# Prompt attention of a hybrid decoder layer: heads in groups of 4, 2, 1 and 1, the causal mask added by a product, ScalarE making all copies of turned probabilities

## Chip, cores and metric

The kernel runs on one core of one Trainium2 chip. The metric is the device time of one execution in microseconds, as the median of several runs.

## The reference, cut to what matters

One layer of a decoder is computed for a prompt of 512 tokens and for 8 sample tokens with a paged past. For the prompt, 16 heads (8 of a latent attention with 96 query values, 8 of a forgetting attention with 64) attend causally over at most 512 keys:

```python
qb = min(Q_BLOCK, T)                       # 128 queries at a time, 4 blocks
...
mask = k_pos[None, :] <= pos[:, None]
s = jnp.where(mask[None, None], s, NEG_INF)
p = jax.nn.softmax(s, axis=-1)
return jnp.einsum('bhqs,bshd->bqhd', p.astype(v.dtype), v)
```

After it come two norms, the output projection, and an expert layer that gathers rows of two large tables. All arithmetic is float32.

## The kernel before, in words

The five engines run programs written out by hand, with a semaphore for each kind of step; within one engine the order of the code is the order of the work. The stages are: projections and attention of the sample rows and of the four prompt blocks b = 0 to 3 (up to about 431 us of the profile), then output projection, routing, and the gathers of expert rows (GpSimd starts each gather, VectorE and TensorE use the rows), with the work on the paged past of the sample tokens between them.

For each prompt block TensorE projects the normed rows (line 1368), turns queries and keys into QT and KT (line 1412), and then goes through 16 heads. For block b there are w = 128(b+1) keys. A head costs:

- scores (line 1422): one float32 product with w columns into PSUM bank 2 or 3, in turn by the head's number. Each float32 product appears as two MATMUL instructions; a transpose appears as one.
- VectorE adds the causal mask to the last 128 columns (line 976, followed by a wait of the engine for itself) and takes the negated row maximum (line 978).
- ScalarE takes the exponential with the maximum as its bias, and sums the row in the same instruction (line 614). It goes to Pm, two buffers.
- TensorE turns the probabilities, b+1 transposes of 128x128, into bank 4 or 5 (line 1430).
- the turned probabilities are copied to SBUF into PT, two buffers: for even heads by VectorE (line 972), for odd heads by ScalarE (line 607).
- values (line 1437): b+1 products with 64 columns, two instructions each, into banks 0 and 1.

TensorE's order is: scores of head hh+1, turn of head hh, values of head hh-1. ScalarE's order is: exponential of hh, and then the copy of hh-1 when that head is odd. VectorE's is the same with mask, maximum and copies of even heads.

Between the heads of blocks 0 to 2 lies a part of the next block's start: x_squares(t+1) on ScalarE after head 4 (line 552), x_mean(t+1) on VectorE after head 5, rms (two small activations, lines 542 and 543) on ScalarE after head 6, x_scale(t+1) on VectorE after head 7 (lines 831 to 834 and 868; it waits for rms), turn_x(t+1) on TensorE after head 10 (8 transposes, line 1349), x_gain(t+1) on VectorE after head 12 (line 875). Block 3 has none of these.

When block 3's last values are done (semaphore o_ps), SyncE loads the last five of eight pieces of w_o (line 403), for which the output projection waits.

Of the kernel before, what the change touches and what calls it, by code (L numbers as in the profile page):

```python
# [18 lines left out]
ALU = mybir.AluOpType  # L19
ACT = mybir.ActivationFunctionType  # L20
AX = mybir.AxisListType
# [4 lines left out]
P = 128  # L26
# [3 lines left out]
NB = T // P  # L30
# [7 lines left out]
VD = 64  # L38
R = 128
FD = 64  # L40
KM = NOPE + RP
KF = FD + 2
# [14 lines left out]
CW = PAST // NCH  # L57
K_V0, K_U1, K_V1, K_U2 = range(0, 12), range(12, 36), range(36, 52), range(52, 64)
V_U2, V_V2, V_U3 = range(0, 6), range(6, 16), range(16, NPG)

TAIL_QPE, TAIL_CKV, TAIL_KPE, TAIL_F = 0, 256, 384, 416
TAIL = 424
# [4 lines left out]
C_ID, C_MASK, C_TRI, C_ONES, C_COS, C_SIN, C_DIM, C_IOTA, C_END = 0, 128, 256, 384, 512, 592, 672, 706, 722  # L67
# [4 lines left out]
def build(nc, x_prompt, x_sample, w_in, w_k, w_v, w_kT, w_o, w_q, sub_keys, gains, g_cols, g_ffn, consts, dec_consts,  # L72
# [3 lines left out]
    with ctx:  # L76
# [3 lines left out]
        def sem(name):  # L80
            return ctx.enter_context(nc.semaphore(name))
# [26 lines left out]
        Pm = part(160, 1024).rearrange("p (i n) -> p i n", i=2)  # L108
        PT = part(164, 1024).rearrange("p (i n) -> p i n", i=2)
# [71 lines left out]
        con = sb("con", [P, C_END])  # L181
# [13 lines left out]
        nmx = sb("nmx", [P, 16])  # L195
        rs = sb("rs", [P, 16])
# [13 lines left out]
        ps = ctx.enter_context(nc.psum_tensor("ps", [P, 8, 512], F32))  # L210
        ident = con[:, C_ID:C_ID + P]
# [49 lines left out]
        s_ps = sem("s_ps")  # L261
        max_done = sem("max_done")
        exp_done = sem("exp_done")
        pT_ps = sem("pT_ps")
        pT_done = [sem("pT_done_even"), sem("pT_done_odd")]
        o_ps = sem("o_ps")
        mx_done = sem("mx_done")
        mixT_done = sem("mixT_done")
# [85 lines left out]
        def _(sp):  # L354
# [172 lines left out]
        def _(act):  # L527
# [29 lines left out]
            for t, b in enumerate(ORDER):  # L557
# [42 lines left out]
                    nc.scalar.activation(dst, src, ACT.Copy).then_inc(qk_even, 1)  # L600
                w = (b + 1) * P

                def copy_pT(hh):
                    act.wait_ge(pT_ps, 16 * b + hh + 1)
                    if 16 * b + hh >= 2:
                        act.wait_ge(o_ps, 16 * b + hh - 1)
                    nc.scalar.activation(PT[:, hh % 2, 0:w], ps[:, 4 + hh % 2, 0:w],
                                         ACT.Copy).then_inc(pT_done[1], 1)

                for hh in range(16):  # L610
                    act.wait_ge(max_done, 16 * b + hh + 1)
                    if 16 * b + hh >= 2:
                        act.wait_ge(pT_ps, 16 * b + hh - 1)
                    nc.scalar.activation(Pm[:, hh % 2, 0:w], ps[:, 2 + hh % 2, 0:w], ACT.Exp,
                                         bias=nmx[:, hh:hh + 1], accum_out=rs[:, hh:hh + 1]
                                         ).then_inc(exp_done, 1)
                    if hh and (hh - 1) % 2:
                        copy_pT(hh - 1)

                    if t < NB and hh == 4:  # L620
                        x_squares(t + 1)
                    if t < NB and hh == 6:
                        rms(P, 1)
                copy_pT(15)
                act.wait_ge(mx_done, b + 1)
                act.wait_ge(o_ps, 16 * (b + 1))
# [187 lines left out]
        def _(dve):  # L814
# [9 lines left out]
            def step(ins):  # L824
                dve.wait_ge(v_step, after(ins))
# [59 lines left out]
            for t, b in enumerate(ORDER):  # L885
# [79 lines left out]
                    V_.tensor_copy(dst, src).then_inc(qk_odd, 1)  # L965
                w = (b + 1) * P

                def copy_pT(hh):
                    dve.wait_ge(pT_ps, 16 * b + hh + 1)
                    if 16 * b + hh >= 2:  # L970
                        dve.wait_ge(o_ps, 16 * b + hh - 1)
                    V_.tensor_copy(PT[:, hh % 2, 0:w], ps[:, 4 + hh % 2, 0:w]).then_inc(pT_done[0], 1)

                for hh in range(16):
                    dve.wait_ge(s_ps, 16 * b + hh + 1)
                    step(V_.tensor_tensor(ps[:, 2 + hh % 2, b * P:w], ps[:, 2 + hh % 2, b * P:w],
                                          con[:, C_MASK:C_MASK + P], ALU.add))
                    V_.tensor_reduce(nmx[:, hh:hh + 1], ps[:, 2 + hh % 2, 0:w], AX.X, ALU.max,
                                     negate=True).then_inc(max_done, 1)
                    if hh and (hh - 1) % 2 == 0:  # L980
                        copy_pT(hh - 1)

                    if t < NB and hh == 5:
                        x_mean(t + 1)
                    if t < NB and hh == 7:
                        x_scale(t + 1)
                    if t < NB and hh == 12:
                        x_gain(t + 1)
                dve.wait_ge(o_ps, 16 * (b + 1))
# [352 lines left out]
        def _(pe):  # L1342
# [19 lines left out]
            for t, b in enumerate(ORDER):  # L1362
# [52 lines left out]
                pe.wait_ge(qk_odd, 4 * (b + 1))  # L1415
                w = (b + 1) * P

                def scores(hh):
                    kd = KM if hh < 8 else KF
                    if hh >= 2:  # L1420
                        pe.wait_ge(exp_done, 16 * b + hh - 1)
                    T_.matmul(ps[:, 2 + hh % 2, 0:w], QT[0:kd, hh, :], KT[0:kd, hh, 0:w],  # L1422
                              start=True, stop=True).then_inc(s_ps, 1)

                def turn(hh):
                    pe.wait_ge(exp_done, 16 * b + hh + 1)
                    if hh >= 2:
                        pe.wait_ge(pT_done[hh % 2], 8 * b + hh // 2)
                    for a in range(b + 1):
                        last = T_.transpose(ps[:, 4 + hh % 2, a * P:(a + 1) * P], Pm[:, hh % 2, a * P:(a + 1) * P],  # L1430
                                            ident)
                    last.then_inc(pT_ps, 1)

                def values(hh):
                    pe.wait_ge(pT_done[hh % 2], 8 * b + hh // 2 + 1)
                    for a in range(b + 1):
                        last = T_.matmul(ps[:, hh // 8, VD * (hh % 8):VD * (hh % 8) + VD],  # L1437
                                         PT[:, hh % 2, a * P:(a + 1) * P], V[:, a, VD * hh:VD * hh + VD],
                                         start=(a == 0), stop=(a == b))
                    last.then_inc(o_ps, 1)  # L1440

                scores(0)
                for hh in range(16):
                    if hh + 1 < 16:
                        scores(hh + 1)
                    turn(hh)
                    if hh:
                        values(hh - 1)
                    if t < NB and hh == 10:
                        turn_x(t + 1)  # L1450
                values(15)
            turn_mixture(NB - 1)


# [465 lines left out]
```

## Time and profile before

| | |
|---|---|
| median of 3 runs | 2458.63 us (2458.03 to 2470.38) |
| span of the profiled execution, first to last instruction | 2563.8 us |
| PE (TensorE matmul) busy | 1793.9 us, 70% |
| DVE (VectorE) busy | 1169.1 us, 46% |
| ACT (ScalarE) busy | 348.5 us, 14% |
| mean granted clock of TensorE | 0.817 of full speed |

Of the profiled execution the span is all that was recorded; no time of its own stands beside it. It is 105 us longer than the median of the runs without a profile. In the profile PE is the matmul part of TensorE and PEld its weight loads, which lie beside matmuls. A granted clock of 1.00 is 2.4 GHz, one of 0.50 is 1.2 GHz.

### The profile page before, as it was taken

The page shows a single profiled execution, that of the slowest core. Times are in us where ns is not written, and L with a number is a line of the kernel's source. Part 1 is how long each engine was busy: PE and PEld are TensorE (multiplying, and loading weights), DVE is VectorE, ACT ScalarE, POOL GpSimd, SP SyncE. Part 2 cuts the span into 40 slices and gives each one's busy share as a digit, 9 for nine tenths or more (in the row PEclk, how much of TensorE's full clock was granted, in tenths as well). Part 3 has the DMA queues.
Part 4 walks back from the last instruction along what each step waited for, and adds up shares of the span by engine and source line. Part 5 has one row for each costly group of instructions (what it writes and reads, how often), then busy time and mean ns, then how long its engine had stood idle before and what let it go on. Part 6 is the DMA issues. An engine that isn't in the chain of part 4 may idle for free.

```text
span 2563.8 us, 31875 instructions
## 1 busy us (share of the span) xinstructions
PE 1793.9 (70%) x11105; PEld 728.5 (28%) x11105; DVE 1169.1 (46%) x2804; ACT 348.5 (14%) x744; POOL 1190.8 (46%) x1076
## 2 busy tenths in 40 slices
PE   6788788855376999988399987631777523227878
PEld 1446445622232343333133332210111100001212
DVE  2334434499822702655680024765800155561352
ACT  1113213100011121322021212200000000000000
POOL 0000000046613656865665565688655444484673
PEclk9876888977689999999599997855899955557997
DMA  4000006069938999999999998999999999999995
GB/s 193 20 9 18 10 1 247 17 251 384 373 131 313 384 399 390 399 393 379 342 331 397 402 382 287 370 365 404 399 405 405 408 405 404 404 392 377 342 352 215
DMA packets 254251, 775.33 MB, mean 302 GB/s; under 512 B 36513, under 2 KB 45370, under 8 KB 250762
## 3 DMA queue, kind: packets, MB, share of 16 engines
q0 software_dynamic: 150784, 547.43, 55.3%
q1 hardware_dynamic: 102138, 221.64, 23.3%
q10 hardware_dynamic: 1168, 4.23, 0.4%
q8 instruction: 87, 1.43, 0.2%
q14 instruction: 74, 0.61, 0.1%
HBM read 766.36 MB, written 6.81 MB: 302 GB/s over the span
## 4 chain that ended last, share of the span: by engine, by line
PE 44%; DMA 24%; issue 12%; DVE 8%; POOL 5%; another core or an unknown queue 3%; ACT 2%; SPq 1%; DVEq 0%; POOLq 0%; ACTq 0%
DMA arena<-peer_v,idxT 14%; PE ps L1562 9%; PE ps L1624 9%; DMA arena<-peer_u,eidx 8%; PE ps L1368 7%; POOL arena L475 5%; PE ps L1610 3%; PE ps L1491 3%; PE ps L1640 2%; DVE arena L1176 2%; PE ps L1422 2%; DMA arena<-kpe_pool 2%; PE ps L1437 1%; PE ps L1412 1%
## 5 line engine op out<-in xcount | busy, mean ns | idle before, releaser
L475 POOL DMA_INDIRECT arena<-peer_u,eidx x512 | 622.2, 1215 | 872.5 <-DVE eidx L1086 512.8
L475 POOL DMA_INDIRECT arena<-peer_v,idxT x512 | 515.0, 1006 | 452.1 <-PE ps L1562 345.5
L1176 DVE CUSTOM_DVE_ANT_0 arena<-arena 128x1024 f32<-128x1024 f32 x384 | 467.0, 1226 | 529.9 <-DMA arena<-peer_u,eidx 457.7
L1562 PE MATMUL ps<-arena 128*32 128x512 f32 x2048 | 554.4, 632 | 125.9 <-DMA arena<-peer_v,idxT 112.5
L1624 PE MATMUL ps<-arena 128*128 128x512 f32 x512 | 303.4, 676 | 15.8 <-DMA arena<-kpe_pool 13.5
L1694 PE MATMUL ps<-arena 128*32 128x512 f32 x512 | 118.0, 874 | 236.5 <-DMA arena<-vn_pool 236.5
L1562 PEld LDWEIGHTS ps<-arena 128*32 128x32 f32 x2048 | 102.9, 111 | 441.0 <-DMA arena<-peer_v,idxT 321.1
L728 ACT ACTIVATE arena<-ps 128x512 f32<-128x512 f32 x256 | 150.0, 596 | 572.3 <-PE ps L1624 240.0
L1610 PE MATMUL ps<-arena 128*32 128x128 f32 x2048 | 177.1, 286 | 44.6 <-issue 35.6
L1368 PE MATMUL ps<-arena 128*128 128x512 f32 (+3 forms) x400 | 174.4, 597 | 6.9 <-DVE arena L952 6.6
L1176 DVE CUSTOM_DVE_ANT_0 arena<-arena,ps 128x1024 f32<-128x1024 f32 x128 | 151.4, 1219 | 11.4 <-DMA arena<-peer_u,eidx 5.3
L1610 PEld LDWEIGHTS ps<-arena 128*32 128x32 f32 x2048 | 85.8, 111 | 178.6 <-issue 156.8
L1640 PE MATMUL ps<-arena 128*32 128x128 f32 x2048 | 103.8, 286 | 36.0 <-issue 35.4
L1207 DVE TENSOR_SCALAR arena<-arena 128x512 f32<-128x512 f32 x8 | 3.4, 426 | 241.5 <-ACT arena L742 236.4
L1624 PEld LDWEIGHTS ps<-arena 128*128 128x128 f32 x512 | 80.6, 196 | 73.2 <-issue 55.5
L1368 PEld LDWEIGHTS ps<-arena 128*128 128x128 f32 (+1 forms) x400 | 69.4, 175 | 107.8 <-issue 107.3
L1640 PEld LDWEIGHTS ps<-arena 128*32 128x32 f32 x2048 | 72.6, 113 | 90.7 <-issue 79.9
L1694 PEld LDWEIGHTS ps<-arena 128*32 128x32 f32 x512 | 17.1, 128 | 257.3 <-issue 137.0
L750 ACT ACTIVATE arena<-ps 128x128 f32<-128x128 f32 x32 | 8.9, 277 | 512.3 <-PE ps L1672 414.9
L1491 PE MATMUL ps<-arena,hb 128*128 128x512 f32 x128 | 60.4, 630 | 2.3 <-issue 1.2
L1422 PE MATMUL ps<-arena 96*128 96x128 f32 (+7 forms) x128 | 58.1, 549 | 3.5 <-DVE arena L965 3.5
L1465 PE MATMUL ps<-arena 128*128 128x512 f32 x128 | 56.8, 605 | 1.7 <-DMA arena<-w_o 1.7
(305 smaller groups left out, 1712.1 us busy)
## 6 DMA issues: line engine op xcount, KB each, us to landing
arena<-kt_pool SPq DMA_DIRECT2D x256, 320.0 KB
arena<-vn_pool SPq DMA_DIRECT2D x256, 320.0 KB
arena<-w_q SPq DMA_DIRECT2D x16, 1024.0 KB, 19.5
arena<-w_in SPq DMA_DIRECT2D x8, 1236.0 KB, 15.9
arena<-w_o SPq DMA_DIRECT2D x16, 512.0 KB, 6.9
arena<-peer_u,eidx POOLq DMA_INDIRECT x512
arena<-peer_v,idxT POOLq DMA_INDIRECT x512
arena<-kpe_pool SPq DMA_DIRECT2D x256, 16.0 KB
```

Source lines behind the costliest of these rows:

```text
L475: pool.indirect_dma_start(ring[:, q % RING, :], None, table, bass.IndirectOffsetOnAxis(ap=index, axis=0)).then_inc(g[q % RING], 16)
L728: nc.scalar.activation(sqd[:, m % 2, :], ps[:, 2 + m % 2, :], ACT.Square).then_inc(sqd_done, 1)
L1176: V_.tensor_tensor_reduce(rows, rows, x, 1.0, 0.0, ALU.mult, ALU.add, acc[:, k:k + 1]).then_inc(u_used, 1)
L1368: ins = T_.matmul(ps[0:n, i, 0:w], xnT[:, c, 0:n], win[:, c, 512 * i:512 * i + w], start=(c == 0), stop=(c == DC - 1))
L1422: T_.matmul(ps[:, 2 + hh % 2, 0:w], QT[0:kd, hh, :], KT[0:kd, hh, 0:w], start=True, stop=True).then_inc(s_ps, 1)
L1465: last = T_.matmul(ps[:, OPB[b] + i, :], mixT[:, b, c, :], wo[:, c, 512 * i:512 * i + 512], start=(c == 0), stop=(c == DC - 1))
L1491: last = T_.matmul(ps[:, 2 + i, :], xT2[b][:, c * P:(c + 1) * P], wq[:, c, 512 * i:512 * i + 512], start=(c == 0), stop=(c == DC - 1))
L1562: return T_.matmul(ps[32 * j:32 * j + 32, i, :], W32[:, j, c, :], ring[:, q % RING, 512 * i:512 * i + 512], start=(c == 0), stop=(c == 31) ...
L1610: last = T_.matmul(ps[32 * j:32 * j + 32, 4 + s % 2, 2 * P:3 * P], dcon[:, E_HM + 32 * (4 * par + q):E_HM + 32 * (4 * par + q) + 32], sqd[ ...
L1624: T_.matmul(ps[:, 2 + m % 2, :], wkd[:, q * P:(q + 1) * P], kbuf[:, slot, :, 512:640], start=True, stop=True).then_inc(n_ps, 1)
L1640: T_.matmul(ps[32 * j:32 * j + 32, 4 + s % 2, 0:P], qz[:, c, 2 * j + par, :], kbuf[:, slot, j, c * P:(c + 1) * P], start=(par == 0 and c = ...
L1694: T_.matmul(ps[32 * j:32 * j + 32, 4 + par, :], pTd[:, s % 2, 32 * j:32 * j + 32], kbuf[:, slot, j, 0:512], start=False, stop=True, tile_p ...
```

## The change

A group is m = 4, 2, 1, 1 heads in blocks 0, 1, 2, 3; the scores of a group fill m times w columns of one bank (512, 512, 384, 512), and there are 4, 8, 16 and 16 groups. Semaphores count groups. The mask is added by TensorE, with a product of the identity and the mask into the same columns. The maximum is one reduction per group with m results. There is still one exponential per head. All copies of turned probabilities are ScalarE's, one per group. The parts of the next block's start now hang on the group: x_squares and x_mean after group NG/4, rms and x_scale after group NG/2, turn_x after 5NG/8, x_gain after 3NG/4.

```diff
+HPG = [4, 2, 1, 1]
+NG = [16 // m for m in HPG]
+GB = [sum(NG[:b]) for b in range(NB)]
+NGROUPS = sum(NG)
...
-        pT_done = [sem("pT_done_even"), sem("pT_done_odd")]
+        pT_done = sem("pT_done")
...
-            sp.wait_ge(o_ps, 16 * NB)
+            sp.wait_ge(o_ps, NGROUPS)
...
+                def copy_pT(gi):
+                    G, m = GB[b] + gi, HPG[b] * w
+                    act.wait_ge(pT_ps, G + 1)
+                    if G >= 2:
+                        act.wait_ge(o_ps, G - 1)
+                    nc.scalar.activation(PT[:, G % 2, 0:m], ps[:, 4 + G % 2, 0:m], ACT.Copy).then_inc(pT_done, 1)
+                for gi in range(NG[b]):
+                    G = GB[b] + gi
+                    act.wait_ge(max_done, G + 1)
+                    if G >= 2:
+                        act.wait_ge(pT_ps, G - 1)
+                    for j in range(HPG[b]):
+                        hh = HPG[b] * gi + j
+                        last = nc.scalar.activation(Pm[:, G % 2, j * w:(j + 1) * w], ps[:, 2 + G % 2, j * w:(j + 1) * w],
+                                                    ACT.Exp, bias=nmx[:, hh:hh + 1], accum_out=rs[:, hh:hh + 1])
+                    last.then_inc(exp_done, 1)
+                    if gi:
+                        copy_pT(gi - 1)
+                    if t < NB and gi == NG[b] // 4:
                         x_squares(t + 1)
+                    if t < NB and gi == NG[b] // 2:
                         rms(P, 1)
...
-                def copy_pT(hh):
...
-                    V_.tensor_copy(PT[:, hh % 2, 0:w], ps[:, 4 + hh % 2, 0:w]).then_inc(pT_done[0], 1)
...
-                    step(V_.tensor_tensor(ps[:, 2 + hh % 2, b * P:w], ps[:, 2 + hh % 2, b * P:w],
-                                          con[:, C_MASK:C_MASK + P], ALU.add))
...
+                for gi in range(NG[b]):
+                    G, m = GB[b] + gi, HPG[b]
+                    dve.wait_ge(s_ps, G + 1)
+                    V_.tensor_reduce(nmx[:, m * gi:m * gi + m], heads(ps[:, 2 + G % 2, 0:m * w], P, m), AX.X, ALU.max,
                                      negate=True).then_inc(max_done, 1)
+                    if t < NB and gi == NG[b] // 4:
                         x_mean(t + 1)
+                    if t < NB and gi == NG[b] // 2:
                         x_scale(t + 1)
+                    if t < NB and gi == 3 * NG[b] // 4:
                         x_gain(t + 1)
...
+                def scores(gi):
+                    G = GB[b] + gi
+                    if G >= 2:
+                        pe.wait_ge(exp_done, G - 1)
+                    for j in range(HPG[b]):
+                        hh = HPG[b] * gi + j
+                        kd = KM if hh < 8 else KF
+                        T_.matmul(ps[:, 2 + G % 2, j * w:(j + 1) * w], QT[0:kd, hh, :], KT[0:kd, hh, 0:w],
+                                  start=True, stop=False, skip_group_check=True)
+                        last = T_.matmul(ps[:, 2 + G % 2, j * w + b * P:(j + 1) * w], ident, con[:, C_MASK:C_MASK + P],
+                                         start=False, stop=True, skip_group_check=True)
+                    last.then_inc(s_ps, 1)
...
+                    for a in range(HPG[b] * (b + 1)):
+                        last = T_.transpose(ps[:, 4 + G % 2, a * P:(a + 1) * P], Pm[:, G % 2, a * P:(a + 1) * P], ident)
...
+                for gi in range(NG[b]):
+                    if gi + 1 < NG[b]:
+                        scores(gi + 1)
+                    turn(gi)
+                    if gi:
+                        values(gi - 1)
+                    if t < NB and gi == 5 * NG[b] // 8:
                         turn_x(t + 1)
```

The values of a group are the same products as before, head by head, after one wait for the group's copy.

## Rows read from the trace of the kernel before

**Rows 1.** The page: its head.
```profile
span 2563.8 us, 31875 instructions
```
**Rows 2.** Windows, the head loops of blocks 0 to 3; columns in the first line.
```profile
core 0: us, PE busy (x) PEld busy (x) DVE busy (x) ACT busy (x) POOL busy (x), PEclk, DMA share, GB/s
121.50:146.30 24.80, 20.84 (x89) 17.71 (x90) 13.70 (x49) 9.94 (x44) 0.00 (x0) 0.58 0.08 22
205.50:240.00 34.50, 31.79 (x137) 27.24 (x138) 16.52 (x48) 12.66 (x44) 0.00 (x0) 0.63 0.05 16
298.10:335.40 37.30, 34.59 (x185) 25.64 (x186) 20.04 (x48) 15.01 (x44) 0.00 (x0) 0.86 0.00 1
393.20:431.00 37.80, 36.04 (x224) 26.70 (x224) 20.65 (x41) 16.45 (x40) 0.00 (x0) 1.00 0.67 276
```
**Rows 3.** Chain of waits, blocks 1 and 3: start us, us, what.
```profile
229.62 1.71 PE ps L1349 x8
...
260.33 0.87 PE ps L1349 x8
...
407.08 0.84 PE ps L1437 x8
407.92 0.91 PE ps L1422 x2
```
**Rows 4.** Timeline, start us, us: steps of blocks 0, 1, 2 and 3.
```profile
127.37 1.05 ACT L552 ACTIVATE arena<-hb 128x1024 f32<-128x1024 f32 x1
...
139.91 0.37 ACT L614 ACTIVATE arena<-ps,nmx 128x128 f32<-128x128 f32 x1 [2.68 <-DVE nmx L978]
...
210.07 0.47 ACT L614 ACTIVATE arena<-ps,nmx 128x256 f32<-128x256 f32 x1 [1.76 <-DVE nmx L978]
...
313.17 0.75 DVE L868 TENSOR_SCALAR hb<-hb,rv 128x1024 f32<-128x1024 f32 x1
...
393.23 1.96 PE L1422 MATMUL ps<-arena 96*128 96x512 f32 x4 [0.87 <-DVE arena L965]
...
394.36 0.30 DVE L976 TENSOR_TENSOR ps<-ps,con 128x128 f32<-128x128 f32 x1 [1.28 <-PE ps L1422]
...
395.42 0.69 ACT L614 ACTIVATE arena<-ps,nmx 128x512 f32<-128x512 f32 x1 [2.87 <-DVE nmx L978]
...
396.25 0.66 PE L1430 MATMUL ps<-con,arena 128*128 128x128 f32 x4 [1.07 <-ACT arena L614]
```
**Rows 5.** Groups by line: x count, busy us, mean ns of one, idle before.
```profile
L978 DVE TENSOR_REDUCE nmx<-ps 128x1 f32<-128x512 f32 x16 | 11.1, 692 | 0.5
...
L607 ACT ACTIVATE arena<-ps 128x512 f32<-128x512 f32 x8 | 4.7, 588 | 0.7 <-PE ps L1430 0.7
...
L893 DVE TENSOR_REDUCE ssv<-arena 128x8 f32<-128x512 f32 (+1 forms) x15 | 9.3, 676 | 75.0 <-ACT arena L569 75.0
```
**Rows 6.** Windows inside blocks 0 to 2, columns as in rows 2.
```profile
204.70:207.50 2.80, 1.11 (x5) 0.68 (x4) 1.83 (x5) 0.62 (x3) 0.00 (x0) 0.99 0.00 0
207.50:229.60 22.10, 21.90 (x83) 18.98 (x84) 10.79 (x33) 8.82 (x32) 0.00 (x0) 0.50 0.00 1
...
125.50:146.20 20.70, 18.16 (x76) 15.62 (x75) 11.05 (x39) 8.28 (x37) 0.00 (x0) 0.50 0.10 27
146.20:149.40 3.20, 3.20 (x5) 1.26 (x5) 1.71 (x4) 1.33 (x4) 0.00 (x0) 0.50 0.01 3
305.00:313.00 8.00, 7.94 (x48) 5.35 (x47) 4.91 (x15) 4.86 (x16) 0.00 (x0) 1.00 0.00 0
313.20:315.30 2.10, 1.45 (x10) 0.84 (x8) 2.03 (x5) 0.54 (x2) 0.00 (x0) 1.00 0.00 0
317.00:327.00 10.00, 10.00 (x39) 7.93 (x37) 3.04 (x8) 1.72 (x5) 0.00 (x0) 0.50 0.01 2
```
**Rows 7.** Windows, line 1412 alone (block 1's transposes of queries and keys): PE, PEld, clock.
```profile
198.16:204.70 6.54, 6.54 (x32) 5.74 (x32) 0.55 0.34 93
```
**Rows 8.** Chain of waits after block 3.
```profile
432.77 6.89 DMA arena<-w_o
```

More of the change, by code:

```diff
@@ L601, in _ @@
                 w = (b + 1) * P
-                def copy_pT(hh):
[L604 to L620, printed above, removed]
+                def copy_pT(gi):
[4 more added lines that the diff above has]
+                    nc.scalar.activation(PT[:, G % 2, 0:m], ps[:, 4 + G % 2, 0:m], ACT.Copy).then_inc(pT_done, 1)
@@ L621, in _ @@
                         x_squares(t + 1)
-                    if t < NB and hh == 6:
+                    if t < NB and gi == NG[b] // 2:
                         rms(P, 1)
-                copy_pT(15)
+                copy_pT(NG[b] - 1)
                 act.wait_ge(mx_done, b + 1)
-                act.wait_ge(o_ps, 16 * (b + 1))
+                act.wait_ge(o_ps, GB[b] + NG[b])
                 for i in range(2):
@@ L966, in _ @@
                 w = (b + 1) * P
[L968 to L971, printed above, removed]
-                    V_.tensor_copy(PT[:, hh % 2, 0:w], ps[:, 4 + hh % 2, 0:w]).then_inc(pT_done[0], 1)
-                for hh in range(16):
-                    dve.wait_ge(s_ps, 16 * b + hh + 1)
-                    step(V_.tensor_tensor(ps[:, 2 + hh % 2, b * P:w], ps[:, 2 + hh % 2, b * P:w],
-                                          con[:, C_MASK:C_MASK + P], ALU.add))
-                    V_.tensor_reduce(nmx[:, hh:hh + 1], ps[:, 2 + hh % 2, 0:w], AX.X, ALU.max,
+                for gi in range(NG[b]):
+                    G, m = GB[b] + gi, HPG[b]
+                    dve.wait_ge(s_ps, G + 1)
+                    V_.tensor_reduce(nmx[:, m * gi:m * gi + m], heads(ps[:, 2 + G % 2, 0:m * w], P, m), AX.X, ALU.max,
                                      negate=True).then_inc(max_done, 1)
-                    if hh and (hh - 1) % 2 == 0:
-                        copy_pT(hh - 1)
-                    if t < NB and hh == 5:
+                    if t < NB and gi == NG[b] // 4:
                         x_mean(t + 1)
-                    if t < NB and hh == 7:
+                    if t < NB and gi == NG[b] // 2:
                         x_scale(t + 1)
-                    if t < NB and hh == 12:
+                    if t < NB and gi == 3 * NG[b] // 4:
                         x_gain(t + 1)
-                dve.wait_ge(o_ps, 16 * (b + 1))
+                dve.wait_ge(o_ps, GB[b] + NG[b])
                 step(V_.reciprocal(rs[:, :], rs[:, :]))
@@ L1416, in _ @@
                 w = (b + 1) * P
[L1418 to L1431, printed above, removed]
-                    last.then_inc(pT_ps, 1)
@@ L1434, in values @@
[L1434 to L1439, printed above, removed]
+                def scores(gi):
[10 more added lines that the diff above has]
+                    last.then_inc(s_ps, 1)
@@ new lines, in turn, with values @@
+                def turn(gi):
+                    G = GB[b] + gi
+                    pe.wait_ge(exp_done, G + 1)
+                    if G >= 2:
+                        pe.wait_ge(pT_done, G - 1)
+                    for a in range(HPG[b] * (b + 1)):
+                        last = T_.transpose(ps[:, 4 + G % 2, a * P:(a + 1) * P], Pm[:, G % 2, a * P:(a + 1) * P], ident)
+                    last.then_inc(pT_ps, 1)
+                def values(gi):
+                    G = GB[b] + gi
+                    pe.wait_ge(pT_done, G + 1)
+                    for j in range(HPG[b]):
+                        hh = HPG[b] * gi + j
+                        for a in range(b + 1):
+                            i = j * (b + 1) + a
+                            last = T_.matmul(ps[:, hh // 8, VD * (hh % 8):VD * (hh % 8) + VD],
+                                             PT[:, G % 2, i * P:(i + 1) * P], V[:, a, VD * hh:VD * hh + VD],
+                                             start=(a == 0), stop=(a == b))
@@ L1440, in values @@
                     last.then_inc(o_ps, 1)
                 scores(0)
[L1443 to L1449, printed above, removed]
+                for gi in range(NG[b]):
[5 more added lines that the diff above has]
+                    if t < NB and gi == 5 * NG[b] // 8:
@@ L1450, in _ @@
                         turn_x(t + 1)
-                values(15)
+                values(NG[b] - 1)
             turn_mixture(NB - 1)
```

## The prediction

> **What bounds it now.** I read the page first [rows 1], then windows over the four head loops [rows 2], then the chain of waits through them [rows 3], the timeline for single steps [rows 4], the groups for durations [rows 5], and at last short windows for TensorE's clock [rows 6, 7]. The four loops last 24.8, 34.5, 37.3 and 37.8 us, 134.4 together. The loops run one after the other with nothing else beside them that ends later: the expert gathers begin after them, and after block 3 the chain goes on through the load of w_o [rows 8], which SyncE starts only when the last values are done. So what the loops save or cost moves everything behind them, and I count it whole.
>
> In each loop PE is the busiest, 84, 92, 93 and 95% [rows 2]. But the same 8 transposes take 1.71 us in one place and 0.87 in another [rows 3]: the first stands where the granted clock is 0.50, 1.2 GHz, the second at 2.4. I call one MATMUL instruction of 128 columns a unit: 0.107 us fast, 0.213 slow. A value instruction, of 64 columns, is a unit as well (8 in 0.84), and scores of 512 columns are 8 units (0.91 with the tail) [rows 3]. A head of block b then has 2(b+1) units of scores, b+1 of turns and 2(b+1) of values, and the loop 80(b+1), plus 8 of turn_x in blocks 0 to 2: 88, 168, 248, 320 units, or 9.4, 18.0, 26.5 and 34.2 us fast. Block 3 is nearly that, 37.8. The others are not: the mean clock was 0.58, 0.63 and 0.86 [rows 2]. Block 1 fell to 0.50 after some microseconds in which PE mostly waited (1.11 busy of 2.80 while the first exponential was due [rows 6]), block 0 after the same start, and they stayed there for 22.1 and 20.7 us, though PE was busy in nearly all of block 1's. Block 2 went at 1.00 until VectorE's x_scale held up the maximum (1.45 busy of 2.10), and then 10 us at 0.50 [rows 6]. So three of the four loops are bound by short waits of PE and what these do to its clock.
>
> **The change, part by part.**
>
> *Mask by a product.* It takes 64 additions of 0.30 us [rows 4] and the engine's wait after each, some 0.33 together, from the path scores, mask, maximum, exponential. It adds to PE 2 instructions of 128 columns per head: 32 units in each loop, 3.4 us fast or 6.8 slow, 128 units or 13.7 to 27.3 us in all. No product into part of a filled bank stands in the trace; the lower bound is 1 unit per head, if its loads hide (1.7 us a loop), the upper 4, as for 256 columns (6.8). I take 2, the nearest row being an instruction of the same shape.
>
> *Groups.* The products, exponentials and transposes stay as many. Waits are per group: PE issues 4 heads' scores, then 4 turns, then 8 value instructions in block 0, so an exponential's latency is paid 4 times and not 16. Maximum: one reduction of 512 columns, 0.69 for one result and 0.68 for eight [rows 5]. Exponentials stay 64, of 0.37 us at 128 columns, 0.47 at 256 and 0.69 at 512 [rows 4]. In block 3 the turn starts 0.83 after the exponential began (395.42 to 396.25 [rows 4]), so the row's sum and the signal add 0.14: 0.51 for the last of a group in block 0, 0.61 in block 1.
>
> *Copies.* A copy of 512 is 0.59 on ScalarE [rows 5]. Now it makes all 44 (4 + 8 + 16 + 16 groups). The copy of group g-1 stands in its queue behind the exponentials of group g; values g-1 wait for it, and x_squares and rms stand behind it. VectorE loses its 32 copies, 8 a block; it had time, busy 55% at most [rows 2].
>
> *The next block's start.* x_mean now sits behind maximum NG/4 on VectorE and waits for x_squares, which is behind exponential NG/4 and a copy on ScalarE; x_scale likewise waits for rms in its own group. VectorE can't take the next maximum meanwhile. x_squares is 1.05, x_scale four small steps and 0.75, 1.5 together [rows 4].
>
> Now block by block at the fast clock, a step's result being there 0.27 us after its last column (393.23 and 8 units end at 394.08, VectorE starts at 394.36 [rows 4]).
>
> *Block 0.* 120 units, 12.8 us. A group is 28 units, 3.0 us; ScalarE's part 4 x 0.37 + 0.59 = 2.1. I walk it from the first score. Turn 0 can start at 1.71 + 0.27 + 0.72 + 3 x 0.37 + 0.51 = 4.3, and PE has issued two groups' scores by 3.4: 0.9 idle. Copy 0 and x_squares hold ScalarE to 7.5 and with it x_mean and maximum 2, so turn 2 starts at 10.1 and not at 9.4: 0.7. rms ends at 10.9, x_scale at 12.5, and turn_x, for which PE was free at 11.4, waits 1.1. Maximum 3 and four exponentials follow, to 14.8, with PE free at 13.4: 1.4. With 0.2 for small ones 4.3 idle, 17.1 us. A stall of this kind let the clock fall in block 2 of before [rows 6], so I add 1.4: 18.5, against 24.8.
>
> *Block 1.* 200 units, 21.4 us. A group is 24 units, 2.56; ScalarE's part 0.94 + 0.59. Maximum and exponentials of a group (0.27 + 0.72 + 0.47 + 0.61 = 2.07) fit between its scores and its turn, which lie 2.56 apart. Idle: at the start 1.28 + 2.07 = 3.35 against 2.56, 0.8; at the x parts, with the same walk, 1.2; at the end and behind copies 1.1. 24.5, against 34.5. PE has no stretch as empty as 204.70 to 207.50 in it, hence the fast clock.
>
> *Block 2.* 280 units, 30.0 us. Heads stay single, so per head 17 units, 1.82. The chain from scores g over maximum (0.59), exponential (0.72), copy g-1 (0.53), values g-1 to scores g+2, the steps of 384 columns taken between those of 256 and 512, is 0.27 + 0.59 + 0.72 + 0.53 + 0.64 + 0.86 = 3.6 for two heads: no more than PE needs. Idle 4.0, mostly at x_scale, where the clock may fall as it did; 2 us for that: 36.0, against 37.3.
>
> *Block 3.* 352 units, 37.6 us, start 0.8, end 1.1: 39.5, against 37.8. Here there was nothing to win: the clock was 1.00 and PE full, and the mask's 32 units come on top.
>
> Sum 118.5, against 134.4: 15.9 less. The projections behind blocks 0 and 1 begin at 0.50 (3.2 us of it after block 0 [rows 6]); if they begin at 1.00, up to 1.6 us each; I take 1.0. So 16.9 less. The profiled span is 105 us over the median [rows 1]; I take the difference to hold as it is for the median, as nothing in these loops depends on DMA: 2458.6 - 16.9 = 2441.7.
>
> *Does the clock rise in time?* Each loop is entered after line 1412, 32 transposes and nothing else. In block 1 these ran at mean 0.55, PE busy all the time [rows 7], and the stretch behind them was at 0.99 [rows 6]. So transposes raised it. The Trainium skill says otherwise (TensorE: Matmul & The Clock Gate, Part 4: PE-mode transpose): full clock doesn't engage for transposes, since they don't count as busy in the same way. The trace disagrees. By the page, the turns and the transposes ahead would leave the loops at 1.2 GHz; that is the third rival below.
>
> **Rivals.**
>
> *Part of the clock only* (gain 5 to 12 us, about 2450). Where the clock falls depends on where PE's waits lie in time. If block 0 falls right at its start (25.6 us, 120 slow units) or block 2 for 20 us (+5 to +8), half of the gain goes. For: block 2 of before, the new waits of VectorE for rms in its own group. Against: the loops have fewer waits.
>
> *Nothing arrives at the end* (within 3 us, 2457): w_o or the gathers wait for something else. Against: w_o is started by the last values and takes 6.89 us [rows 8] whenever that is, and the DMA engines were busy for only 0.67 of block 3's loop [rows 2], so what SyncE had issued before it was over by then.
>
> *Slower: the mask's products on a slow engine.* PE stays at 0.50 in blocks 0 to 2, as it did for 22 us in block 1 with PE full [rows 6]. Then 120, 200 and 280 units cost 25.6, 42.7 and 59.7, with block 3 167.5 in all, 33 more: 2492. With block 3 at 39.5, it decides where the first three loops pass 94.9; all fast they are 75.6, all slow 128, so at somewhat over a third of the way. For: PE busy with heads didn't raise the clock in block 1, and the mask's units cost double there. Against: it was entered fast, and what made it fall was the wait at its start, which is now 0.8.
>
> *The product doesn't replace the addition cheaply*: 4 units a head give 13.7 us more at the fast clock, gain 3, 2455.
>
> **Numbers.** The forecast, gain 12 to 23: 0.62. Part of the clock: 0.20. Nothing arrives: 0.04. Dear product: 0.05. Slower: 0.09. The range: low end, block 0 at 17.1, block 1 at 24.2, block 2 at 34, block 3 at 38.9, and 3 for projections, 23 less, and 3 for the scatter of runs: 2432. High end: the partial case, 2450, with a dear product on top of it, 13.7: 2464. Half a per cent (12.3 us), about what a measurement of this kernel can tell from no change, cuts through the partial case: faster 0.61 of the forecast and 0.04 of the partial case, 0.65; slower the third rival and 0.01 for a dear product on a slow engine, 0.10; same the rest, 0.25.
>
> **What would show it.** Block 0's window 17 to 20 us, block 1's near 24.5 at a clock above 0.9, block 2's 34 to 38, block 3's 38.9 to 41; two new instructions of 0.11 us each per head at the fast clock; PE's wait before the first turn below 1 us; the longest waits of PE beside x_scale. Wrong if the clock of block 1 stays at 0.5 to 0.6, if a mask product takes over 0.3 us at the fast clock, or if the loops shorten and the time between block 3 and the first gather grows.

## The result and the profile after

The changed kernel takes 2447.51 us (median of 6 runs, 2445.9 to 2451.42), the kernel before 2459.88 (6 runs, 2458.03 to 2470.38): 12.4 us less. The ratio is 0.994 with a 95% interval of 0.9921 to 0.996, so 10 to 19 us less, with the ratio itself at 15. The forecast was 16.9 less, in a range down to 2432 and up to 2464. Half a per cent, the step that the forecast called faster (12.3 us), lies inside this interval: that the kernel is faster is clear, that it is faster by that much is not.

The page after, its head and the busy times:

```profile
span 2444.7 us, 31973 instructions
...
PE 1721.6 (70%) x11233; PEld 710.9 (29%) x11233; DVE 1134.7 (46%) x2688; ACT 357.4 (15%) x756; POOL 1175.3 (48%) x1076
```

PE is busy for 70% of the span as before, VectorE for 34 us less. The span of before's profiled execution was 119 us longer [rows 1], while the medians differ by 12. So the two spans must not be set against each other. The attention part can: it is the same stretch of work in both, its code outside the head loops is unchanged, and between the loops the two profiles differ by 2.0 us in 175. Windows over the four head loops after, from the first score to the last value, answer to [rows 2]:

```profile
120.90:139.82 18.92, 16.47 (x121) 15.65 (x122) 5.41 (x12) 9.42 (x40) 0.00 (x0) 0.87 0.09 29
198.26:222.88 24.62, 23.19 (x169) 21.50 (x170) 8.17 (x16) 13.50 (x44) 0.00 (x0) 1.00 0.08 23
280.22:317.97 37.75, 35.40 (x217) 29.72 (x218) 11.38 (x24) 18.08 (x52) 0.00 (x0) 0.91 0.00 1
375.54:415.65 40.11, 39.27 (x256) 31.08 (x256) 11.06 (x16) 20.37 (x48) 0.00 (x0) 1.00 0.66 272
```

The columns are those of rows 2 (span of the window, busy time of PE, PEld, DVE, ACT and POOL with the number of instructions, granted clock, DMA share, GB/s). Measured in the same way (first score to last value) the loops of before are 24.6, 34.4, 37.3 and 37.7, 134.0 together; after they are 18.9, 24.6, 37.8 and 40.1, 121.4. The clock went from 0.58 to 0.87 and from 0.63 to 1.00 in the first two. PE issues 32 instructions more in each loop, and in block 3, where the clock was full before, the loop is 2.4 us longer. VectorE's busy time fell (20.65 to 11.06 in block 3), ScalarE's rose (16.45 to 20.37); neither is near the loop's length.

From the first score of block 0 to the last value of block 3 it is 309.4 us before and 294.8 after: 14.6 less, of which 12.6 in the loops and 2.0 between them. The chain at the end of block 3, beside [rows 8]:

```profile
413.81 1.84 PE ps L1445 x16
...
417.47 6.88 DMA arena<-w_o
```

w_o is again what follows the last values, with 6.88 us as before with 6.89. So 12.6 of the 14.6 us were made in the loops, and the load of w_o, which comes next, took nothing back. What lies behind it can't be compared in these two profiles; the times, 10 to 19 us apart, leave no room for a loss of more than 5 us there.

### The profile page after: what moved, and what is told of

The parts are those of the page before. It is cut to its first block, busy times and chain, and to the rows that moved or that the text cites. A ratio compares the mean times of both kernels' runs of the same rounds, so it can differ in the third digit from the quotient of the medians.

```text
span 2444.7 us, 31973 instructions
## 1 busy us (share of the span) xinstructions
PE 1721.6 (70%) x11233; PEld 710.9 (29%) x11233; DVE 1134.7 (46%) x2688; ACT 357.4 (15%) x756; POOL 1175.3 (48%) x1076
## 4 chain that ended last, share of the span: by engine, by line
DMA 33%; PE 32%; DVE 11%; issue 10%; POOL 8%; SPq 4%; ACT 1%; DVEq 0%; POOLq 0%; ACTq 0%
DMA arena<-peer_u,eidx 16%; DMA arena<-peer_v,idxT 16%; POOL arena L479 8%; PE ps L1570 8%; PE ps L1366 7%; PE ps L1632 5%; DVE arena L1174 4%; SPq L441 2%; PE ps L1618 2%; SPq L438 1%; PE ps L1445 1%; PE ps L1423 1%; PE ps L1648 1%; PE ps L1492 1%; PE ps L1811 1%
## 5 line engine op out<-in xcount | busy, mean ns | idle before, releaser
L479 POOL DMA_INDIRECT arena<-peer_u,eidx x512 | 606.0, 1183 | 860.3 <-DVE eidx L1084 498.2
L1570 PEld LDWEIGHTS ps<-arena 128*32 128x32 f32 x2048 | 103.4, 111 | 415.8 <-DMA arena<-peer_v,idxT 326.0
L1618 PE MATMUL ps<-arena 128*32 128x128 f32 x2048 | 165.2, 284 | 1.8 <-ACT arena L735 1.8
L1174 DVE CUSTOM_DVE_ANT_0 arena<-arena,ps 128x1024 f32<-128x1024 f32 x128 | 152.5, 1218 | 19.2 <-DMA arena<-peer_u,eidx 16.7
L1618 PEld LDWEIGHTS ps<-arena 128*32 128x32 f32 x2048 | 83.4, 110 | 129.9 <-issue 118.8
L1702 PEld LDWEIGHTS ps<-arena 128*32 128x32 f32 x512 | 17.0, 128 | 259.4 <-issue 139.3
L1648 PE MATMUL ps<-arena 128*32 128x128 f32 x2048 | 87.4, 283 | 0.0
L1648 PEld LDWEIGHTS ps<-arena 128*32 128x32 f32 x2048 | 68.2, 112 | 44.6 <-issue 32.5
```

The source lines that it names most:

```text
L479: pool.indirect_dma_start(ring[:, q % RING, :], None, table, bass.IndirectOffsetOnAxis(ap=index, axis=0)).then_inc(g[q % RING], 16)
L1174: V_.tensor_tensor_reduce(rows, rows, x, 1.0, 0.0, ALU.mult, ALU.add, acc[:, k:k + 1]).then_inc(u_used, 1)
L1570: return T_.matmul(ps[32 * j:32 * j + 32, i, :], W32[:, j, c, :], ring[:, q % RING, 512 * i:512 * i + 512], start=(c == 0), stop=(c == 31) ...
L1618: last = T_.matmul(ps[32 * j:32 * j + 32, 4 + s % 2, 2 * P:3 * P], dcon[:, E_HM + 32 * (4 * par + q):E_HM + 32 * (4 * par + q) + 32], sqd[ ...
L1648: T_.matmul(ps[32 * j:32 * j + 32, 4 + s % 2, 0:P], qz[:, c, 2 * j + par, :], kbuf[:, slot, j, c * P:(c + 1) * P], start=(par == 0 and c = ...
L1702: T_.matmul(ps[32 * j:32 * j + 32, 4 + par, :], pTd[:, s % 2, 32 * j:32 * j + 32], kbuf[:, slot, j, 0:512], start=False, stop=True, tile_p ...
```

## The experiments

All times of loops are from first score to last value, each from one profiled execution. Every kernel but the filler is an edit of the changed kernel. The runs were made at different times, each beside the kernel before, so whole times are compared by their ratio to it. Five runs (each product twice, copies shared, the product taken away in both executions, the changed kernel once more) have a single time: it is given, but only their loops bear on the argument.

**Mask back on VectorE.** `MASK_PE` is False for all four blocks, and the product is issued only where it is True:

```diff
+                    if not MASK_PE[b]:
+                        own = heads(ps[:, 2 + G % 2, 0:m * w], P, m)[:, :, b * P:w]
+                        step(V_.tensor_tensor(own, own, con[:, C_MASK:C_MASK + P].unsqueeze(1).to_broadcast([P, m, P]),
+                                              ALU.add))
...
-                        last = T_.matmul(ps[:, 2 + G % 2, j * w + b * P:(j + 1) * w], ident, con[:, C_MASK:C_MASK + P],
-                                         start=False, stop=True, skip_group_check=True)
```

> The changed kernel with the mask back on VectorE, one addition per group over its heads. Theory (short waits of PE and what they do to its clock decide; the product costs its two units a head and buys that the waits stay short): block 3 goes back to 37 to 38 us from 40.1, but blocks 0 to 2 get slower: block 0 about 20, block 1 26 to 31, block 2 38 to 50, each with a longer stretch at granted clock 0.50; sum 125 to 137 against 121.4 of the changed kernel. Rival (grouping alone makes the gain, and the product is pure cost): all four loops get shorter by the product's units, 3.4 us each, and the sum is about 108 to 110, 12 us under the changed kernel.

Its four windows:

```profile
121.37:140.14 18.77, 16.61 (x89) 16.05 (x90) 8.11 (x16) 9.29 (x40) 0.00 (x0) 0.64 0.10 29
196.41:223.42 27.01, 21.64 (x137) 18.85 (x138) 11.32 (x24) 13.28 (x44) 0.00 (x0) 0.94 0.07 20
280.69:319.06 38.37, 33.45 (x185) 24.57 (x186) 15.88 (x40) 18.05 (x52) 0.00 (x0) 0.91 0.00 1
376.30:414.06 37.76, 36.09 (x224) 26.67 (x224) 15.76 (x32) 20.35 (x48) 0.00 (x0) 1.00 0.68 281
```

The sum is 121.9 against 121.4, below the range that the theory gave and far from the rival's 108 to 110. The product costs 2.4 us in block 3 and brings 2.4 in block 1, where the clock fell without it (0.94); blocks 0 and 2 hardly move. The difference of the sums, 0.5, is less than the 2.0 by which the changed kernel differs from itself (below), so as the change stands no worth of the product is shown. In block 0 the clock fell to a mean of 0.64 without the product, yet the loop was not longer than the changed kernel's at 0.87. Two differences cancel there. Up to the last turn it took 15.4 us against 14.5. Behind that, the same instructions took 3.4 us against 4.4, because here the clock rose again before the end, while in the changed kernel it had just fallen. The time, 2451.8 us (ratio to before 0.9962, 0.9942 to 0.9982), fits the loops: its interval overlaps with the changed kernel's.

**Groups of one head.**

```diff
-HPG = [4, 2, 1, 1]
+HPG = [1, 1, 1, 1]
```

> The changed kernel with groups of one head in every block: mask by the product and all copies by ScalarE stay. Theory: blocks 2 and 3 are the same code as in the changed kernel, 36 to 38 and 40 us; blocks 0 and 1 lose their grouping: 22 to 24.5 and 27 to 30.5 us, so the sum is about 128, between before (134.0) and the changed kernel (121.4). Rival (the product alone, by taking VectorE's step out of the chain and filling PE, holds the clock up, and grouping adds nothing): blocks 0 and 1 as in the changed kernel, 18.9 and 24.6.

```profile
120.73:142.70 21.97, 17.90 (x121) 16.03 (x122) 6.93 (x24) 11.32 (x52) 0.00 (x0) 0.92 0.09 26
199.11:228.08 28.97, 25.77 (x169) 23.40 (x170) 9.06 (x24) 14.62 (x52) 0.00 (x0) 0.94 0.07 20
284.46:318.90 34.44, 32.09 (x217) 26.92 (x218) 11.38 (x24) 18.06 (x52) 0.00 (x0) 1.00 0.01 1
```

Blocks 0 and 1 came as expected. Against the changed kernel they lose 3.1 and 4.4 us, which is what grouping is worth, with what it does to the clock (0.94 for 1.00 in block 1). Against before they still gain 2.7 and 5.4, which the product, the copies and the clock bring without it, not told apart here. Block 2, whose code is the same as in the changed kernel, took 34.4, below the 36 to 38 expected, and not 37.8: there the clock did not fall. The sum is 125.5, where about 128 was expected. The ratio, 0.9971 (0.9954 to 0.9989; 2453.3 us), stands behind the changed kernel's 0.994 as the sums do, 125.5 and 121.4, though the two intervals overlap a little.

**Filler in the kernel before.** Products whose result nobody reads, in waits of PE:

```diff
                     if hh + 1 < 16:
                         scores(hh + 1)
+                    if (b == 0 and hh <= 10) or hh == 0:
+                        T_.matmul(ps[:, 6, 0:256 if b == 0 else 512], ident, con[:, 0:256 if b == 0 else 512],
+                                  start=True, stop=True)
```

> The kernel before with products added that nobody reads: one of 512 columns in PE's wait before the first turn of blocks 1 to 3, and one of 256 columns per head in heads 0 to 10 of block 0. It computes the same. Theory (the clock makes most of the loss of blocks 0 and 1): PE stays at 1.00 in nearly all of block 1, which goes from 34.4 to 26.5 to 28.5 us with more work on PE than before; block 0 goes from 24.6 to 20.5 to 23; blocks 2 and 3 unchanged within 1, or block 2 moved by where its own fall comes. Rival (the number of waits decides, and the clock only follows from them): block 1 stays above 32 us, and block 0 gets longer by its filler, 25 to 27.

```profile
121.77:143.68 21.91, 17.94 (x111) 14.65 (x112) 13.31 (x48) 9.95 (x44) 0.00 (x0) 0.92 0.09 25
202.96:232.21 29.25, 25.49 (x139) 19.74 (x140) 16.70 (x48) 12.44 (x44) 0.00 (x0) 0.88 0.06 19
291.64:327.60 35.96, 34.14 (x187) 24.99 (x188) 19.94 (x48) 15.00 (x44) 0.00 (x0) 0.91 0.00 0
384.59:422.31 37.72, 36.91 (x226) 27.05 (x226) 20.63 (x40) 16.47 (x40) 0.00 (x0) 1.00 0.69 285
```

This is the run that shows the clock by itself. Two instructions more in block 1 (139 for 137) went with a loop 5.2 us shorter, 34.4 to 29.2, its clock 0.88 for 0.63; block 0 went from 24.6 to 21.9 with 22 more instructions. Nothing else was changed: heads, waits and order are those of before. Block 1 missed its range (26.5 to 28.5) by 0.7, as the clock still fell, but 15 us into the loop and not 2; block 2, 36.0, moved by 1.3. Each kernel stands here with one profile, but the mean clock of whole executions says the same: 0.834 (0.831 to 0.838) in ten with the filler, 0.829 (0.825 to 0.834) in 25 of before. The loops sum to 124.8, 9.2 less, and the time is 2455.3 us, ratio 0.9981 (0.9962 to 0.9999), 0.2 to 9 us less: work that nobody needs made the kernel no slower, and by the interval a little faster.

**VectorE's parts of the next block one group later.**

```diff
-                    if t < NB and gi == NG[b] // 4:
+                    if t < NB and gi == NG[b] // 4 + 1:
                         x_mean(t + 1)
-                    if t < NB and gi == NG[b] // 2:
+                    if t < NB and gi == NG[b] // 2 + 1:
                         x_scale(t + 1)
...
-                    if t < NB and gi == 5 * NG[b] // 8:
+                    if t < NB and gi == max(5 * NG[b] // 8, NG[b] // 2 + 1):
                         turn_x(t + 1)
```

> The changed kernel with x_mean and x_scale on VectorE one group later, as they stood relative to ScalarE's parts before the change (turn_x in block 0 also one group later). Theory (VectorE waits in its own group for ScalarE, and the next maximum stands behind it): block 0 loses 1 to 2 us of PE's waits, 17 to 18.5 us against 18.9; block 2 36 to 37 against 37.75, with its fall of the clock gone or shorter; block 1 24 to 24.6; block 3 has no such parts, 40.1. Sum 118 to 120.5. Rival (what ends PE's wait there is ScalarE's queue with x_squares and the copies, wherever VectorE's part stands): no loop moves by more than 0.5 us.

```profile
121.06:136.59 15.53, 13.95 (x120) 13.42 (x120) 5.01 (x12) 9.35 (x40) 0.00 (x0) 1.00 0.01 2
194.88:218.60 23.72, 22.64 (x169) 21.39 (x170) 8.23 (x16) 13.50 (x44) 0.00 (x0) 1.00 0.08 23
274.79:307.13 32.34, 31.45 (x217) 26.80 (x218) 11.46 (x24) 18.15 (x52) 0.00 (x0) 1.00 0.00 1
363.42:403.53 40.11, 39.27 (x256) 31.09 (x256) 11.07 (x16) 20.34 (x48) 0.00 (x0) 1.00 0.69 285
```

The first theory had the cause and missed the size: 111.7 us, 9.7 less than the changed kernel's 121.4 (7.7 less than its second execution), where 1 to 3.4 less was expected. The clock is 1.00 in all four loops. The time is 2438.2 us, ratio to before 0.9921 (0.9894 to 0.9948): 13 to 26 us less than before, while its interval and that of the changed kernel still overlap. In block 0 the edit moves TensorE's turn_x as well, by one group. The timeline of VectorE in block 0, first the changed kernel, then this one:

```profile
128.54 0.15 DVE L870 TENSOR_SCALAR ssv<-ssa 128x1 f32<-128x1 f32 x1 [3.10 <-ACT arena L556]
128.61 0.68 DVE L978 TENSOR_REDUCE nmx<-ps 128x4 f32<-128x512 f32 x1
131.68 0.16 DVE L838 TENSOR_TENSOR tv<-r0v 128x1 f32<-128x1 f32 x1 [2.39 <-ACT r0v L547]
...
132.45 0.75 DVE L875 TENSOR_SCALAR hb<-hb,rv 128x1024 f32<-128x1024 f32 x1
133.12 0.68 DVE L978 TENSOR_REDUCE nmx<-ps 128x4 f32<-128x512 f32 x1
```

```profile
127.88 0.69 DVE L978 TENSOR_REDUCE nmx<-ps 128x4 f32<-128x512 f32 x1 [2.28 <-PE ps L1425]
128.69 0.15 DVE L870 TENSOR_SCALAR ssv<-ssa 128x1 f32<-128x1 f32 x1
130.99 0.69 DVE L978 TENSOR_REDUCE nmx<-ps 128x4 f32<-128x512 f32 x1 [2.15 <-PE ps L1425]
131.60 0.15 DVE L838 TENSOR_TENSOR tv<-r0v 128x1 f32<-128x1 f32 x1
```

In the changed kernel VectorE sat 3.10 us on x_squares (line 556) with the maximum of group 2 behind it, and 2.39 us on rms (line 547) with the maximum of group 3 behind x_scale. Not all of that was lost: counted from the first score, the two maxima started at 7.7 and 12.2 us, and here at 6.8 and 9.9. One group later the maxima end VectorE's idle time with PE's scores, and the sums of ScalarE are there when VectorE comes to them.

**The best version: the same, and block 3's mask on VectorE.**

```diff
+MASK_PE = [True, True, True, False]
```

> The kernel with VectorE's parts one group later (111.7 us in its four loops) and, besides, the mask of block 3 added by VectorE again. Theory (in block 3 PE is full at the fast clock and the product's 32 units lie on its path, while VectorE's addition does not): block 3 takes 37.4 to 38.1 us against 40.1, blocks 0 to 2 unchanged within 0.7; sum 109 to 110. Rival (VectorE's step in the chain costs as much as PE's two units): block 3 stays at 39.5 or above.

```profile
363.40:401.17 37.77, 36.08 (x224) 26.73 (x224) 15.77 (x32) 20.37 (x48) 0.00 (x0) 1.00 0.72 297
```

As the theory said: block 3 is 37.8 and the others repeat within 0.02 us; the sum is 109.4. The time is 2434.59 us (median of 6, 2431.72 to 2438.43), ratio to before 0.99 (0.9877 to 0.9923). It beats the kernel before by 19 to 30 us. All its times lie below all of the changed kernel's, which were taken at another time; the intervals of the two ratios just touch.

**Each product twice.**

```diff
                         last = T_.matmul(ps[:, 2 + G % 2, j * w + b * P:(j + 1) * w], ident, con[:, C_MASK:C_MASK + P],
+                                         start=False, stop=False, skip_group_check=True)
+                        last = T_.matmul(ps[:, 2 + G % 2, j * w + b * P:(j + 1) * w], ident, con[:, C_MASK:C_MASK + P],
                                          start=False, stop=True, skip_group_check=True)
```

> The changed kernel with every mask product issued twice; masked scores are then -2e30 and the result is the same. It prices the product. Theory (2 units of 0.107 us per product at the fast clock, on PE's path wherever PE is full): block 3 40.1 + 3.4 = 43.5 us, block 1 24.6 + 2.5 to 3.5, block 0 within 1 of 18.9 and block 2 36 to 40, as there PE has waits to fill and the clock can go either way. Rival (a product into a part of a filled bank is dearer than its columns): block 3 at 45 or more; or cheaper, with loads hidden: 41.8 or less.

```profile
121.46:140.22 18.76, 17.57 (x153) 17.13 (x154) 5.41 (x12) 9.40 (x40) 0.00 (x0) 1.00 0.10 29
196.82:223.66 26.84, 26.20 (x201) 24.96 (x202) 8.18 (x16) 13.49 (x44) 0.00 (x0) 1.00 0.07 20
281.19:318.07 36.88, 35.60 (x249) 30.50 (x250) 11.47 (x24) 18.15 (x52) 0.00 (x0) 1.00 0.00 1
374.49:417.95 43.46, 42.85 (x288) 34.66 (x288) 11.07 (x16) 20.34 (x48) 0.00 (x0) 1.00 0.61 253
```

Block 3 went from 40.11 to 43.46: 3.35 us for 32 instructions, 0.105 each, so a product into part of a filled bank costs its two units where PE is full. The first 32 had cost only 2.35 there (37.76 to 40.11), as PE had room while VectorE added the mask: its idle time went from 1.67 to 0.84. Block 1 paid 2.2. Block 0 is 18.8 us at a clock of 1.00 with 153 instructions, as it was at 0.87 with 121 and at 0.64 with 89. That looks like a bound which neither work nor clock moves, but it is a coincidence. The end of the loop, from the last turn to the last value, first the changed kernel, then this one:

```profile
135.40:139.82 4.42, 4.42 (x21) 4.42 (x22) 0.28 (x1) 1.03 (x2) 0.00 (x0) 0.50 0.38 120
```

```profile
137.74:140.22 2.48, 2.48 (x21) 2.41 (x22) 0.28 (x1) 1.03 (x2) 0.00 (x0) 1.00 0.59 197
```

Up to the last turn the added products cost 1.8 us (16.3 against 14.5). Behind it the same 21 instructions took 1.9 less, because the clock had not fallen. Block 2 was 36.9 us: shorter than the changed kernel's 37.8, where the clock fell, and 2.4 longer than the 34.4 of the single heads, where it did not. The one time of this kernel is 2458.2 us.

**Copies shared again**, with VectorE's parts one group later:

```diff
+                    if gi and (gi - 1) % 2 == 0:
+                        copy_pT(gi - 1)
...
-                    if gi:
+                    if gi and (gi - 1) % 2:
                         copy_pT(gi - 1)
```

The first hunk is VectorE's, with a copy function of its own, the second ScalarE's; the semaphore is again one for even and one for odd groups.

> The kernel with VectorE's parts one group later, and the copies of turned probabilities shared again: even groups by VectorE, odd ones by ScalarE. Theory (ScalarE has time for all copies once nothing else stands ahead of them): no loop moves by more than 0.6 us, sum 111 to 113. Rival (the copies on ScalarE are a part of the gain, since VectorE's copy delays the next maximum): blocks 0 to 2 get 1 to 4 us longer each and a clock falls below 0.95. Third reading (ScalarE's queue is what remains): blocks 0 and 1 get shorter by 0.5 to 1.5 us.

The loops took 15.4, 23.7, 32.6 and 40.1 us at a clock of 1.00, 111.8 against 111.7. With VectorE's parts placed so, it makes no difference to the loops which engine makes the copies; with the changed kernel's placing this was not tested. The one time is 2442.0 us.

**The product alone taken away**, with VectorE's parts one group later, and the same once more.

> The kernel with VectorE's parts one group later and the mask added by VectorE in all blocks: the product alone taken away from it. Theory (with the stalls at the next block's parts gone the clock holds without the product too, but the addition lengthens the chain where a group's chain is already as long as PE's work): block 0 16.5 to 18.5 us against 15.5, block 1 24 to 26 against 23.7, block 2 32 to 36 against 32.3, block 3 37.4 to 38.1; sum 110 to 117. Rival (the product is what keeps PE dense enough for the fast clock): block 0 or block 2 has a clock below 0.9 and the sum is above 117.

```profile
120.98:141.33 20.35, 17.58 (x89) 17.21 (x90) 8.12 (x16) 9.30 (x40) 0.00 (x0) 0.60 0.03 7
199.59:224.21 24.62, 21.72 (x137) 18.86 (x138) 11.45 (x24) 13.39 (x44) 0.00 (x0) 0.92 0.08 22
283.41:316.15 32.74, 30.50 (x185) 22.01 (x186) 16.09 (x40) 18.16 (x52) 0.00 (x0) 1.00 0.01 1
372.98:410.74 37.76, 36.09 (x224) 26.64 (x224) 15.76 (x32) 20.35 (x48) 0.00 (x0) 1.00 0.69 287
```

> The kernel with VectorE's parts one group later and the mask by VectorE in all blocks, profiled once more: block 0 was 20.4 us at a mean clock of 0.60 there. Theory (without the product block 0's groups leave PE so empty that its clock falls in any execution): block 0 again at 19 us or more and below 0.75. Rival (it was one unlucky execution): block 0 under 17.5 us at 0.95 or more.

```profile
123.92:143.14 19.22, 16.46 (x88) 15.95 (x88) 7.62 (x16) 9.29 (x40) 0.00 (x0) 0.64 0.00 1
```

Neither theory for the first run was right. Block 0 was outside the first one's range and had the low clock of the rival, and the sum, 115.5, stayed under the rival's 117. The second run repeats block 0, 19.2 us at 0.64. So in block 0 the product is worth 3.7 to 4.8 us once VectorE no longer stalls: without it, in both executions, the clock falls. In block 1 it brought 0.9 us against the first execution and cost 0.5 against the repeat (23.2, and 23.7 with it), in block 2 it brought 0.4 in both, and in block 3 it costs 2.4. In sum it is worth 3.8 and 1.2 us (115.5 and 112.9 against 111.7). The single times are 2443.4 and 2442.5 us.

**The changed kernel once more.**

> The changed kernel, unchanged, profiled once more. Block 2's code is the same in it and in the kernel with single heads, yet it took 37.75 us there (mean clock 0.91) and 34.44 here (1.00). Theory (the same short waits end in a fall of the clock in some executions and not in others): blocks 1 and 3 repeat within 0.3 us, 24.6 and 40.1, while blocks 0 and 2 may differ, 17 to 19.5 and 34 to 38, each with its clock: block 2 at 1.00 means under 35. Rival (the time before block 2, set by blocks 0 and 1, fixes it): all four loops repeat within 0.3 us.

```profile
122.92:141.57 18.65, 16.21 (x121) 15.33 (x122) 5.41 (x12) 9.40 (x40) 0.00 (x0) 0.90 0.10 30
200.82:225.43 24.61, 23.18 (x169) 21.50 (x170) 8.17 (x16) 13.48 (x44) 0.00 (x0) 1.00 0.08 23
282.91:318.98 36.07, 33.73 (x217) 28.41 (x218) 11.38 (x24) 18.07 (x52) 0.00 (x0) 0.95 0.00 1
375.77:415.88 40.11, 39.27 (x256) 31.10 (x256) 11.06 (x16) 20.35 (x48) 0.00 (x0) 1.00 0.68 281
```

Blocks 1 and 3, whose clock never fell, repeat to 0.01 us; block 2 was 36.1 and not 37.8, and block 0 18.7 and not 18.9. The same program differs by 2.0 us in these loops by how long the clock is low after a stall. So it is the first theory that holds; its last part, a block 2 at 1.00, did not occur. The one time is 2451.8 us, beside 2457.4 for before.

## Why the prediction was right, and where not

*What bounds.* Right, and for block 1 the filler shows it: with the heads of before untouched, a fuller PE in the wait at the start of block 1 gave back 5.2 us. That wait, 1.11 us busy of 2.80 [rows 6], was the cause named.

*Block 0*: 18.5 forecast, 18.9 and 18.7 measured. The walk held step by step, counted from the first score at 120.90; the turns and turn_x of the changed kernel on PE:

```profile
125.25 0.66 PE L1435 MATMUL ps<-con,arena 128*128 128x128 f32 x4 [0.54 <-ACT arena L621]
...
130.89 0.66 PE L1435 MATMUL ps<-con,arena 128*128 128x128 f32 x4
...
133.26 1.09 PE L1347 MATMUL ps<-con,hb 128*128 128x128 f32 x8 [0.78 <-DVE hb L875]
135.40 0.90 PE L1435 MATMUL ps<-con,arena 128*128 128x128 f32 x3 [1.05 <-ACT arena L621]
```

Turn 0 at 4.35 (forecast 4.3), turn 2 at 9.99 (10.1), turn_x at 12.36 (12.5), turn 3 at 14.5 (14.8). The clock fell behind that last stall, as was allowed for, with 1.4 us; by the 4.42 and 2.48 of the product issued twice it cost 1.9:

```profile
131.20:135.00 3.80, 2.37 (x20) 1.93 (x17) 2.60 (x8) 1.58 (x10) 0.00 (x0) 1.00 0.00 0
135.10:141.80 6.70, 6.40 (x23) 5.34 (x24) 2.12 (x4) 1.66 (x5) 0.00 (x0) 0.50 0.25 81
```

*Block 1*: 24.5 forecast, 24.6 twice. PE's idle time before the first turn was 0.52 us, and the clock stayed up.

*Block 2*: 36.0 forecast, 37.8 and 36.1 measured, 34.4 where the clock held. The idle time of 4.0 was 4.4 (34.4 less the 30.0 of work), and the 2 us for a fall were 3.3 and 1.6: whether the clock falls in this block, and for how long, differs between executions of the same code, so how near 36.0 came is partly luck. In the profiled run the fall was the longer one, 6.7 us at 0.50 after 4.14 busy of 5.20:

```profile
296.10:301.30 5.20, 4.14 (x30) 3.35 (x29) 2.82 (x8) 2.56 (x9) 0.00 (x0) 1.00 0.00 0
302.30:309.00 6.70, 6.70 (x28) 5.79 (x27) 0.76 (x2) 1.05 (x3) 0.00 (x0) 0.50 0.00 0
```

*Block 3*: 39.5 forecast, 40.1 in both executions. The idle time of 1.9 was 2.5.

*Sum and end*: 118.5 forecast, 121.4 and 119.4. Between the loops 1.0 was taken and 2.0 measured. Together 14.6 less up to the last value, where 16.9 was forecast; the term that was too good is block 2, with 1.8 of the 2.9. The interval of the ratio, 10 to 19 us, holds both. Its lower part belongs to the rival of a partial gain (5 to 12 us) too, and block 2 did a part of what that rival described; what speaks against it is the clock of 1.00 in all of block 1 and 14.6 us in the profile.

*The mask's product*: two units, as taken; the dear product of the rivals is refuted by 0.105 us per instruction. But the text let the product stand as a price for shorter waits, and the sum of its terms could not show what it bought: with VectorE's stalls in place, taking it away changed the sum by 0.5 us.

*The placing of the next block's parts* was named as a cost, and the walk of block 0 gave it 3.2 us (0.7, 1.1 and 1.4) beside 1.4 for the clock. Taking it away gave 3.4 in block 0, 0.9 in block 1 and 3.7 to 5.4 in block 2. Of the 3.4, about 1.9 is the clock and 1.5 the waits, so the walk had the stalls at twice what could be won back. In block 2 it is 2.1 for the waits (34.4 to 32.3, both at 1.00) and the rest the clock. The expectation for the experiment, 1 to 3.4 in sum, was too timid, since the falls of the clock went with the stalls.

*The slower rival* did not come near. All loops were entered at the full clock, and what TensorE had just done was transposes alone. In the changed kernel too, block 1's began at 0.50, and the window with the last of them and the wait for the first scores stood at 1.00:

```profile
196.50:198.20 1.70, 0.94 (x9) 0.66 (x6) 1.37 (x2) 0.59 (x1) 0.00 (x0) 1.00 0.00 0
```

By the Trainium skill (TensorE: Matmul & The Clock Gate, Part 4: PE-mode transpose) the full clock doesn't engage for transposes; the trace shows that here it did.

## What to carry to other kernels

Where the granted clock of a stage is below 1.00, look for the engine's short waits ahead of each fall before counting its work: here two added instructions saved 5 us in a loop, and steps moved behind the next group's work saved 8 to 10 over the four loops. A step that waits for another engine should stand one iteration after the step it waits for, not beside it, whenever something on the critical path is queued behind it. Work moved onto the busiest engine pays only in those stages where that engine has waits: once those stalls were gone, the mask's product was worth 4 to 5 us in block 0 and cost 2.4 in block 3.

## What the runs showed that I had not expected

- Block 0 took 18.8, 18.9 and 18.8 us with 89, 121 and 153 PE instructions at mean clocks of 0.64, 0.87 and 1.00. The three equal lengths suggest one bound and have none in common: up to the last turn it was 15.4, 14.5 and 16.3 us, and behind it 3.4, 4.4 and 2.5, by the clock at that moment. A mean over a loop hides when the clock was low.
- More work came with a shorter loop: block 1 of before with 2 instructions more (34.4 to 29.2). And the same 32 instructions, the mask's product, were worth 3.7 to 4.8 us in block 0 and cost 2.4 in block 3.
- Loops at a clock of 1.00 repeat to 0.02 us between kernels (15.53 and 15.55, and 40.11 in four of them), while those in which it fell differ with the same code by 0.3 us (block 0 of the changed kernel), 1.1 (block 0 without the product) and 1.7 (block 2 of the changed kernel).
